# Block compression on four column groups of TensorE, with a new order of the small steps, in a two-block transformer kernel

## The reference, cut to what matters

```python
def compress_blocks(x, pe, w1, w2):            # x: 256 tokens, 2 groups of 64 features
    ...
    blk = jnp.concatenate([ch[:, j:j + n_c] for j in range(r)], axis=2)   # 15 windows of 32 tokens
    blk = blk + pe[None, None, :, None, :].astype(x.dtype)
    h = jax.nn.gelu(jnp.einsum('bnlgd,ldf->bngf', blk, w1.reshape(CMP_BLOCK, D, CMP_HIDDEN)))
    return jnp.einsum('bngf,fd->bngd', h, w2)
```

## Time and profile before

| | us |
|---|---|
| median of 3 runs (lowest 1143.5, highest 1143.5) | 1143.5 |
| the profiled execution, its own time | 1144.46 |
| its span, first to last instruction | 1142.7 |
| the span's busy time on TensorE (PE) | 1119.2 |
| first mixer, stages 2 to 17: from about 21 us to 160 us of the span | |

### The profile page before, as it was taken

The page is one execution under the profiler, slowest core; times in us unless marked ns, Lnnn a source line. Parts: engine busy times, 40 slices in busy tenths (PEclk is TensorE's granted clock), DMA queues, the critical chain, the costliest instruction groups (busy, mean ns, idle before and its releaser), DMA issues.

```text
span 1142.7 us, 15900 instructions
## 1 busy us (share of the span) xinstructions
PE 1119.2 (98%) x6253; PEld 929.6 (81%) x6253; DVE 831.1 (73%) x1368; ACT 587.0 (51%) x912; POOL 56.8 (5%) x105
## 2 busy tenths in 40 slices
PE   8999999999999999999999999999999998999997
PEld 7767568888878887888888878888879886888886
DVE  6569449878775777698788889877884557656664
ACT  7345445454445675645444674444466566544442
POOL 1101000000000000010000001000011000000000
PEclk9999999999999999999999999999999999999999
DMA  9526259987844334798876279778636443755530
GB/s 337 169 93 226 76 211 369 340 294 274 309 155 147 122 137 165 268 400 310 297 281 239 74 259 408 287 280 301 237 121 230 157 149 98 276 200 199 185 111 37
DMA packets 39578, 252.19 MB, mean 221 GB/s; under 512 B 6744, under 2 KB 6944, under 8 KB 10832
## 3 DMA queue, kind: packets, MB, share of 16 engines
q1 hardware_dynamic: 26928, 189.67, 46.3%
q0 software_dynamic: 12576, 61.51, 14.8%
HBM read 249.37 MB, written 4.25 MB: 222 GB/s over the span
## 4 chain that ended last, share of the span: by engine, by line
PE 87%; DVE 7%; ACT 3%; issue 1%; DMA 1%; POOL 0%; DVEq 0%; ACTq 0%
PE bank L1487 51%; PE bank L1638 25%; PE bank L1931 2%; PE bank L1690 2%; PE bank L1715 1%; PE bank L1753 1%; PE bank L1571 1%; DVE x L922 1%; PE bank L1912 1%; DMA u<-qk 1%; DVE work L920 1%; PE bank L2002 1%; DVE wlo L1051 1%; DVE wlo L899 1%; DVE us L966 0%
## 5 line engine op out<-in xcount | busy, mean ns | idle before, releaser
L899 DVE TENSOR_TENSOR wlo<-raw,whi 128x2048 fp32r<-128x2048 f32 x140 | 319.0, 2283 | 61.2 <-ACT whi L554 61.1
L554 ACT ACTIVATE whi<-raw 128x2048 fp32r<-128x2048 f32 x141 | 267.9, 1904 | 2.4 <-DMA raw<-in_stream 1.5
L1487 PE MATMUL bank<-whi,hh 128*128 128x512 f32 x544 | 214.1, 394 | 0.0
L1487 PE MATMUL bank<-wlo,hh 128*128 128x512 f32 x544 | 212.4, 390 | 0.0
L1487 PE MATMUL bank<-whi,hl 128*128 128x512 f32 x544 | 211.8, 389 | 0.0
L1638 PE MATMUL bank<-us,whi 128*128 128x512 f32 x832 | 197.0, 389 | 0.0
L1638 PEld LDWEIGHTS bank<-us,whi 128*128 128x128 f32 x832 | 156.2, 188 | 32.4
L1487 PE MATMUL bank<-us,whi 128*128 128x256 f32 x880 | 168.0, 291 | 0.0
L1487 PEld LDWEIGHTS bank<-us,whi 128*128 128x128 f32 x880 | 137.7, 192 | 9.0 <-issue 8.2
L1487 PE MATMUL bank<-whi,us 128*128 128x512 f32 (+2 forms) x384 | 122.2, 386 | 5.7 <-DVE us L966 1.6
L625 ACT ACTIVATE hh<-work 128x512 fp32r<-128x512 f32 x56 | 35.4, 633 | 173.3 <-PE bank L1487 173.3
(11 more groups left out here) (239 smaller groups left out, 1172.5 us busy)
## 6 DMA issues: line engine op xcount, KB each, us to landing
raw<-in_stream SPq DMA_DIRECT2D x176, 1024.0 KB, 4.9
qk<-in_w_mod POOLq DMA_DIRECT2D x48, 1024.0 KB, 5.6
bias_rows<-bias_heads POOLq DMA_DIRECT2D x4, 768.0 KB, 17.6
u<-bias_rows POOLq DMA_DIRECT2D x16, 128.0 KB, 2.9
vo<-feature_rows POOLq DMA_DIRECT2D x3, 512.0 KB, 8.8
raw<-in_stream SPq DMA_DIRECT2D x2, 696.0 KB, 8.0
x<-in_x SPq DMA_DIRECT2D x2, 512.0 KB, 4.7
cb<-feature_rows POOLq DMA_DIRECT2D x2, 512.0 KB, 6.6
```

Of the source, the lines that this page charges most:

```text
L554: nc.scalar.activation(whi[:, c % RING, 0:w], raw[:, n % RING, 0:w], ACT.Copy).then_inc(hi_ready, 1)
L899: nc.vector.tensor_tensor(wlo[:, c % RING, 0:w], raw[:, raw_index(c) % RING, 0:w], whi[:, c % RING, 0:w].bitcast(fp32), ALU.subtract).then ...
L1487: ins = mm(out, st, mv, start=start and i == 0, stop=stop and i == 2, skip_group_check=True)
```

## The change

Two parts. First, the eight products of a stage no longer add up in one place: product k goes to the 32 rows of the bank that begin at 32 (k mod 4), which is another group of 32 columns of TensorE's array. The windows are padded from 30 to 32 with zeros (a memset of VectorE). ScalarE copies the 128 x 256 result to SBUF (`part`), and one product with a constant 0/1 matrix of 128 x 30 (`sel`, 30 more columns of the constants) sums the four groups back to 30 rows of the bank (`gather`). The eight products of a stage now stand together, with the steps of quarters 0 and 1 before them and those of 2 and 3 behind. Second, the places in the three tables are new. Below are the code and the rows of the tables of which the text speaks; what else stands in the tables was moved in the same manner.

```diff
+    for r in range(4):
+        con[32 * r + np.arange(2 * NBLK), C_SEL + np.arange(2 * NBLK)] = 1
...
-        blk = uf[:, 1024:1984].rearrange("p (c l n) -> p c l n", c=2, l=16)
+        blk = uf[:, 1024:2048].rearrange("p (c l n) -> p c l n", c=2, l=16)
+        part = [work[:, 0, 256 * kv:256 * kv + 256] for kv in range(2)]
+        sel = con[:, C_SEL:C_SEL + 2 * NBLK]
...
             def gelu_square(kv, b):
+                act.wait_ge(c_sum, kv + 1)
+                nc.scalar.activation(hact[kv], b, ACT.Square).then_inc(g_sq, 1)
+
+            def hidden_parts(kv, b):
                 act.wait_ge(plain_used, 2 * kv + 2)
-                nc.scalar.activation(hact[kv], b, ACT.Square).then_inc(g_sq, 1)
+                nc.scalar.activation(part[kv], b, ACT.Copy).then_inc(c_part, 1)
...
                 dve.wait_ge(kc2_in, 128)
+                nc.vector.memset(blk[:, :, :, 2 * NBLK:32], 0.0)
...
+            def hidden_sum(kv, b):
+
+                pe.wait_ge(c_part, kv + 1)
+                mm(b, sel, part[kv], start=True, stop=True).then_inc(c_sum, 1)
...
+                steps(0)
+                steps(1)
                 for k in range(KB):
-                    if k % 2 == 0:
-                        steps(k // 2)
-                    ins = mm(bank[1 if kv else 6][0:30, 0:256], blk[:, kv, KB * half + k, :], w1[:, k, :],
-                             start=half == 0 and k == 0, stop=half == 1 and k == KB - 1, skip_group_check=True)
+                    r = 32 * (k % 4)
+                    ins = mm(bank[1 if kv else 6][r:r + 32, 0:256], blk[:, kv, KB * half + k, :], w1[:, k, :],
+                             start=half == 0 and k < 4, stop=half == 1 and k >= 4, skip_group_check=True)
                 ins.then_inc(plain_used, 1)
+                steps(2)
+                steps(3)
...
-E_PE = {"swap": {0: (3, 3), 1: (4, 1), 2: (5, 1), 3: (6, 2), 4: (7, 1), 5: (8, 2), 6: (13, 1), 7: (14, 1)},
-        "score": {0: (5, 3), 1: (7, 1), 2: (8, 2), 3: (8, 3), 4: (10, 1), 5: (10, 3), 6: (11, 2), 7: (12, 1), 8: (13, 2),
-            9: (14, 1), 10: (14, 2), 11: (15, 2)},
...
-        "value": {0: (7, 1), 1: (9, 0), 2: (9, 3), 3: (10, 3), 4: (11, 3), 5: (12, 2), 6: (13, 0), 7: (13, 3), 8: (15,
-            0), 9: (15, 2), 10: (16, 0), 11: (16, 2)},
...
-        "index": {0: (7, 3), 1: (8, 1)},
-        "hidden": {0: (10, 3), 1: (13, 0)},
-        "keys": {0: (11, 1)},
-        "scores": {0: (11, 3)},
...
+E_PE = {"swap": {0: (4, 0), 1: (5, 0), 2: (5, 2), 3: (6, 3), 4: (7, 1), 5: (9, 0), 6: (13, 1), 7: (14, 1)},
+        "score": {0: (5, 3), 1: (7, 1), 2: (8, 0), 3: (8, 3), 4: (9, 3), 5: (10, 0), 6: (11, 2), 7: (12, 2), 8: (13, 3),
+            9: (14, 2), 10: (14, 2), 11: (14, 2)},
+        "turn": {0: (6, 3), 1: (8, 0), 2: (8, 3), 3: (9, 0), 4: (9, 2), 5: (9, 3), 6: (9, 3), 7: (10, 1), 8: (11, 2), 9:
+            (11, 2), 10: (12, 0), 11: (12, 0), 12: (12, 2), 13: (12, 3), 14: (13, 2), 15: (13, 3), 16: (14, 1), 17: (14,
+            2), 18: (15, 0), 19: (15, 1), 20: (15, 2), 21: (15, 3), 22: (16, 0), 23: (16, 1)},
+        "value": {0: (8, 3), 1: (9, 1), 2: (10, 0), 3: (10, 3), 4: (11, 3), 5: (12, 2), 6: (13, 0), 7: (14, 0), 8: (15,
+            0), 9: (15, 2), 10: (16, 0), 11: (16, 3)},
...
+        "index": {0: (8, 0), 1: (8, 0)},
+        "hidden": {0: (10, 0), 1: (13, 0)},
+        "keys": {0: (10, 1)},
+        "scores": {0: (10, 3)},
...
+        "gather": {0: (9, 2), 1: (11, 2)},
...
+        "exps": {0: (5, 0), 1: (7, 0), 2: (8, 2), 3: (8, 3), 4: (10, 3), 5: (11, 1), 6: (12, 0), 7: (12, 3), 8: (13, 3),
...
+        "copy": {0: (7, 0), 1: (8, 1), 2: (8, 1), 3: (8, 3), 4: (9, 1), 5: (9, 2), 6: (9, 3), 7: (11, 1), 8: (11, 3), 9:
...
+        "part": {0: (9, 0), 1: (11, 2)},
...
-        "hi": {5: (2, 0), 6: (2, 3), 7: (3, 3), 8: (9, 3), 9: (11, 3), 10: (16, 1), 11: (16, 1)}}
...
+        "hi": {5: (2, 0), 6: (2, 2), 7: (3, 2), 8: (9, 3), 9: (10, 3), 10: (17, 0), 11: (17, 3)}}
...
+        "max": {0: (5, 3), 1: (7, 0), 2: (8, 1), 3: (8, 3), 4: (9, 3), 5: (10, 3), 6: (11, 3), 7: (12, 1), 8: (13, 3),
...
+        "norm": {0: (6, 0), 1: (7, 1), 2: (8, 3), 3: (9, 1), 4: (11, 0), 5: (11, 3), 6: (12, 1), 7: (13, 0), 8: (14, 1),
...
+        "round": {0: (8, 1), 1: (8, 3), 2: (9, 1), 3: (9, 1), 4: (10, 2), 5: (11, 0), 6: (11, 0), 7: (12, 1)},
...
-        "blocks": {0: (5, 0)},
...
+        "blocks": {0: (6, 3)},
+        "inner": {0: (9, 3), 1: (12, 0)},
+        "gelu": {0: (10, 0), 1: (12, 1)},
+        "hidden": {0: (10, 3), 1: (12, 3)},
+        "keys": {0: (11, 0)},
...
+        "lo": {4: (2, 0), 5: (3, 2), 6: (4, 2), 7: (5, 2), 8: (11, 0), 9: (12, 0), 10: (17, 3), 11: (17, 3)}}
```

More of the change, by code:

```diff
@@ L150 @@
[L150 to L160, removed]
-        "exp": {0: (12, 0)},
-        "hi": {5: (2, 0), 6: (2, 3), 7: (3, 3), 8: (9, 3), 9: (11, 3), 10: (16, 1), 11: (16, 1)}}
@@ L163 @@
[L163 to L169, removed]
+E_PE = {"swap": {0: (4, 0), 1: (5, 0), 2: (5, 2), 3: (6, 3), 4: (7, 1), 5: (9, 0), 6: (13, 1), 7: (14, 1)},
[6 more added lines that the diff above has]
+            0), 9: (15, 2), 10: (16, 0), 11: (16, 3)},
+        "add": {0: (13, 3), 1: (13, 3)},
+        "index": {0: (8, 0), 1: (8, 0)},
+        "hidden": {0: (10, 0), 1: (13, 0)},
+        "keys": {0: (10, 1)},
+        "scores": {0: (10, 3)},
+        "probabilities": {0: (13, 0)},
+        "gather": {0: (9, 2), 1: (11, 2)},
+        "values": {0: (13, 1)}}
@@ new lines @@
+E_ACT = {"rope": {0: (3, 1), 1: (3, 2), 2: (4, 3), 3: (5, 1), 4: (6, 2), 5: (9, 1), 6: (13, 2), 7: (14, 0)},
+        "exps": {0: (5, 0), 1: (7, 0), 2: (8, 2), 3: (8, 3), 4: (10, 3), 5: (11, 1), 6: (12, 0), 7: (12, 3), 8: (13, 3),
+            9: (14, 3), 10: (15, 0), 11: (16, 1)},
+        "copy": {0: (7, 0), 1: (8, 1), 2: (8, 1), 3: (8, 3), 4: (9, 1), 5: (9, 2), 6: (9, 3), 7: (11, 1), 8: (11, 3), 9:
+            (11, 3), 10: (11, 3), 11: (12, 2), 12: (12, 2), 13: (12, 2), 14: (13, 1), 15: (13, 2), 16: (14, 1), 17: (14,
+            1), 18: (15, 1), 19: (15, 2), 20: (16, 0), 21: (16, 2), 22: (16, 2), 23: (16, 2)},
+        "take": {0: (11, 1), 1: (14, 1), 2: (15, 3), 3: (17, 3)},
+        "index": {0: (7, 1), 1: (7, 1)},
+        "row": {0: (5, 2)},
+        "part": {0: (9, 0), 1: (11, 2)},
+        "square": {0: (9, 1), 1: (11, 3)},
+        "tanh": {0: (9, 3), 1: (12, 1)},
+        "exp": {0: (12, 0)},
+        "hi": {5: (2, 0), 6: (2, 2), 7: (3, 2), 8: (9, 3), 9: (10, 3), 10: (17, 0), 11: (17, 3)}}
@@ new lines @@
+E_DVE = {"rope": {0: (2, 3), 1: (5, 0), 2: (5, 0), 3: (6, 0), 4: (6, 3), 5: (7, 2), 6: (12, 2), 7: (14, 0)},
+        "max": {0: (5, 3), 1: (7, 0), 2: (8, 1), 3: (8, 3), 4: (9, 3), 5: (10, 3), 6: (11, 3), 7: (12, 1), 8: (13, 3),
+            9: (14, 3), 10: (14, 3), 11: (15, 3)},
+        "norm": {0: (6, 0), 1: (7, 1), 2: (8, 3), 3: (9, 1), 4: (11, 0), 5: (11, 3), 6: (12, 1), 7: (13, 0), 8: (14, 1),
+            9: (15, 1), 10: (15, 3), 11: (17, 1)},
+        "index": {0: (8, 0)},
+        "round": {0: (8, 1), 1: (8, 3), 2: (9, 1), 3: (9, 1), 4: (10, 2), 5: (11, 0), 6: (11, 0), 7: (12, 1)},
@@ L723, in _ @@
                     nc.scalar.activation(oT[c], bank[7][:, :].rearrange("p (b n) -> p b n", b=2), ACT.Copy).then_inc(e_oc, 1)
+                for kv in due(E_ACT, "part", i, q):
+                    hidden_parts(kv, bank[1 if kv else 6][:, 0:256])
                 for kv in due(E_ACT, "square", i, q):
@@ L1888, in steps @@
                         pair_scores("e", p)
+                    for kv in due(E_PE, "gather", i, q):
+                        hidden_sum(kv, bank[1 if kv else 6][0:2 * NBLK, 0:256])
                     for kv in due(E_PE, "hidden", i, q):
```

21 lines of the change are left out of this document (7 added, 14 removed).

## The result

The changed kernel takes 1146.83 us (median of 14 runs, 1144.14 to 1151.33) where the kernel before took 1143.5 (14 runs on the same chip, 1139.19 to 1145.4). The ratio is 1.0041, 95% interval [1.0029, 1.0054]: slower by 0.41%, which is 4.7 us. A kernel's times lie on more than one level, so the two can differ: the medians here are 3.3 us apart.) The forecast was 1141.3 with 1137.2 to 1145.2 as its range; the time lies outside. The profiled execution took 1146.95, with a span of 1145.2 against 1142.7.

A forecast was written before the change was run, and what follows sets the result against it. TensorE (PE) was taken as the bound, VectorE as second limit in the compression. The terms -11.8 - 4.3 + 1.1 + 9.7 + 0.7 - 0.3 + 2.7 = -2.2 us took 1143.5 to 1141.3; range 1137.2 to 1145.2.

The forecast's parts named there:

- rival C: The clock falls in new PE gaps of stages 10 and 14, costing 1.6 us once or twice: 1142.6 to 1144; chance 0.22.
- The old wait: PE's 2.52 us wait at a rope swap before stage 7 and some 1.6 of slow clock go: 4.3 us gained.
- a constant of 1.0: The median was taken to lie 1.0 us below the time of the profiled execution.
- 0.7 - 0.3: Stage 12 gets 0.7 us of waits (turn 11, value 5); an old wait of 0.3 in stage 13 goes.
- Products, -11.8: Compression products in four stages: four column groups run side by side, 0.96 us a stage; 15.6 us become 3.8.
- D: Only two column groups run side by side, 0.87 us more in each stage: 1143.0; chance 0.07.
- E: Groups of 32 columns don't overlap at all, each burst takes 3.56 us: 1148; chance 0.08.
- Added on PE: Two gather products, each a float32 product of 0.53 us, add 1.1 us together.
- memset, queues: VectorE's memset takes 0.2 us, covered ahead of its use; loads and transfers in the DMA queues cost nothing.
- The new waits: PE stands for other engines in stages 8 to 11: 2.0, 2.9, 4.2 and 0.6 us, together 9.7.
- Rival B: VectorE keeps up better than walked: half of the 9.7 us of waits isn't there, 1136.5; chance 0.13.
- Stage 14, +2.7: Scores 9, 10 and 11 in one quarter each wait for the previous one's max: PE stands 2 x 1.37 us.

The follow-up runs named there:

- before, again: The kernel before, unchanged, profiled a second time and timed beside more runs of its own: 1139.75 against 1140.19 us, ratio 0.9996.
- filled through: The changed kernel with idle products in nearly all of PE's waits of stages 8 to 12: 1140.64 us against 1140.09 for the kernel before, ratio 1.0003.
- the same, scores apart: The changed kernel with nearly all those waits filled, and scores 10 and 11 moved to (14, 3) and (15, 0): 1137.63 against 1139.71 us, ratio 0.9976.
- The gap in the old kernel: The kernel before, with turn 5 in stage 9 made to wait for two extra ScalarE copies: 1145.6 against 1139.86 us, ratio 1.0048.
- old places: The four column groups with the three tables of the kernel before, gather and part put in beside: 1139.92 against 1140.56 us, ratio 0.9997.
- one group: The changed kernel's new tables, but all eight products in one column group, without part and gather: 1149.38 us against 1140.56 for the kernel before, ratio 1.0074.
- partly filled: The changed kernel with idle products ahead of steps where PE waits in stages 8 to 10: 1143.54 us against 1140.56 for the kernel before, ratio 1.0019.
- rounds out: The changed kernel without four of eight selection rounds, 6.1 us of VectorE's work: 1147.15 us against 1139.86 for the kernel before, ratio 1.0062.
- scores apart: The changed kernel, unfilled, with scores 10 and 11 moved to (14, 3) and (15, 0): 1145.7 us against 1140.56 for the kernel before, ratio 1.0044.

## Why the prediction was wrong

| | stage 7's last products | stage 12 | stage 14 | mixer's end |
|---|---|---|---|---|
| before, first profile | 66.89 | 98.61 | 121.41 | 160.10 |
| before, again | 63.12 | 94.84 | 117.63 | 156.32 |
| after | 60.16 | 101.53 | 122.74 | 163.94 |
| after, filled through | 60.04 | 94.53 | 115.73 | 156.94 |
| the same, scores apart | 59.96 | 94.45 | 115.66 | 154.39 |

(us of the span: the start of the first record of each stage's large work, and for stage 7 and the mixer's end the start of the last one. What the tables move from one side of a border to the other moves between the columns too.)

**The step that decides: the clock, which the sum has at nothing and rival C sized too small.** The forecast's sum has no term for a fall of the clock; only rival C has one, "once or twice" 1.6 us. It fell once and stayed down for 23.9 us. The price is 163.94 - 156.94 = 7.0 us, read from the changed kernel and its filled twin; all of it lies ahead of stage 12 (100.03 and 93.03). A second reckoning comes near: 21.61 us of products at half clock are 10.8 too long, and 3.3 of that fell into waits (10.4 walked, 7.1 measured), which leaves 7.5. The mechanism was named with a chance of 0.22, and its time, 1142.6 to 1144, came from the single fall in the earlier trace rows. Its places were wrong as well: it looked at stages 10 and 14, the fall began in stage 9, and stage 14 ran at 1.00 in both profiles. I took the length of one fall for that of all. The gap in the old kernel shows that length again (3.4 us, where long products follow); in the new places with short bursts it doesn't hold. Which mixture of small products and waits keeps the clock low stays open: in the profiled executions neither the waits alone (old places: 8.3 us of them, clock 1.00) nor the new tables alone (one group: 3.4 us) do it.

**The step that would have been wrong at full clock too: "The old wait", -4.3 us.** It was in the execution of the first profile, 3.8 us by the mixer's end, but it hangs on when one transfer lands (46.58 or 44.31), and the edit that removes it alone wins nothing in the median (1.0004). Of the five profiled kernels with `blocks` at (5, 0), two have it (2.5 us, and 3.2 in the old places), two have no wait there and one has 0.2. The sum was made against that one execution and then carried to the median by a constant of 1.0. Without this term the sum is +2.1, not -2.2: no gain. The filled twin, in which the clock's price is nil, ends its mixer 0.6 later than the kernel before does without the wait, and has a ratio of 1.0003. Of the 1.5 us between +2.1 and +0.6, 0.5 lie ahead of stage 12, which begins 1.5 us earlier (94.54 to 93.03) where -11.8 + 1.1 + 9.7 = -1.0 was summed. The other 1.0 lies behind it: from there to the mixer's end it is 61.78 us in the kernel before and 63.91 in both the changed kernel and its twin, +2.1 where 0.7 - 0.3 + 2.7 = +3.1 was summed. Small steps that the tables move over that border blur this split, and what in the walk was too dear stays open.

**Products, -11.8: right.** 1.00 us for a stage (0.96 taken). Rivals D and E are out. Four records start together: the profile in a window of 0.1 us of the kernel after shows the first four of one burst

```profile
65.43 0.42 PE L1933 MATMUL bank<-raw,u 128*32 128x256 f32 x4
```

in 0.42 us, as two records of different groups in the earlier trace rows take 0.44. Sixteen by 0.216, which is 3.46, in 1.00 is 3.5 times.

**Added on PE, 1.1, memset, queues: right.** The gather's pair takes 0.62 from start to end, the memset 0.11; no PE wait is put down to a DMA between 60 and 165 us.

**The new waits, +9.7: right up to the fall of the clock,** each to 0.1 us, and right in sum to 0.4 in the filled twin (stage 12 at 93.03 for 92.6). Rival B is out. What they mean I had wrong: "it lies not in the places but in VectorE's load". With 6.1 us of VectorE's work left out stage 12 came no earlier in the new places, and 0.13% was won in the old ones (0.9984 for 0.9997, within the intervals). Moving some of the steps left 7.0 us of waits under other names. My reading of the two is this: the chain score, max, exps, norm, turn, copy, value passes PE, VectorE and ScalarE in turn, and once PE's own work in a stage is short, there is nothing for it to do meanwhile. Shortening 15.6 us of products to 4 takes away the cover under which these small steps ran.

**Stage 14, +2.7: right** (1.37 and 1.35 in the trace; 2.5 us when undone, in both pairs of runs). It was a plain loss, for which nothing was gained elsewhere.

So the sign of the result comes from the clock, and the missing gain from the waits. With the clock held and the scores apart, the same change gives 0.9976; of the 10.7 us of PE work that the four groups save, 1.9 arrive at the mixer's end (156.32 - 154.39).

## What to carry to other kernels

Before booking a gain for a wait, look whether it is there in a second execution; a wait that hangs on a transfer's landing may be in one of two. Shortening products that lie between small dependent steps removes their cover too: what is won is at most the shortening less the waits that open, and here these could be walked from a trace to 0.1 us each. Where PE then stands often and works in short bursts between, price a fall of the clock by nearly all of the stretch up to the next long dense work, at twice the products' time less what falls into waits, not by the one fall that the trace happens to show. Idle products in nearly all the waits held the clock here and cost 0.4 us at most (93.03 for 92.6); with part of the waits filled the clock still fell, for 10.2 us in one profile and 3.4 in another.

## What was not expected of the hardware

The granted clock stayed at its lower level for 23.9 us with PE busy for 21.61 of them, 7.7 of these in one piece. With long products behind the gap it was 3.4 us, in the gapped and in the one-group kernel; in the kernels between, pieces of 10.2 (partly filled), 13.7 (rounds out) and 17.1 us (scores apart) were seen. In all the profiles with a long piece the clock was back 0.7 to 1.9 us before the first projection product of stage 12. Two profiled executions of the changed kernel agree (75.7, 23.9 us), yet some timed runs of it are 3 to 6 us shorter at a higher mean clock, so a median of one kernel covers two or three sorts of execution.

Four groups of 32 columns take 1.00 us for 16 records, 3.5 times one group's pace. The Trainium skill ("TensorE: Matmul & The Clock Gate", on packing small matmuls) states 2.38 times for three groups, at 512 columns where these products have 256. That is 0.79 of the full factor, and 0.86 is measured here with the border of 0.1 us counted in. With four groups of 256 the measurement decides: 1.00 us for a stage, where the page's factor would have made it some 0.2 more than the 0.96 taken.
